# Five reorderings around the waits of TensorE in a two-block forward pass on one core: sums inside units, a chunked tail, split square sums, a double norm, pool products inside attention

## The reference, cut to what matters

```python
def reference(x, mem, ...):
    x = first_block(x, mem, ...)       # recurrence + fox attention, memory attention, MLP, final rmsnorm
    return second_block(x, c_2, ...)   # two layers, below

def second_block(x, c, ada_w, ada_b, ...):
    cond = jax.nn.silu(c)
    for layer in range(2):
        mod = cond @ ada_w[layer] + ada_b[layer]               # the conditioning: 1024 x 6144
        sh1, sc1, g1, sh2, sc2, g2 = jnp.split(mod, 6, axis=-1)
        h = modulate(rms_norm(x), sh1, sc1)
        y = pool_attention_mixer(h, ...) if layer % 2 == 0 else mlstm_mixer(h, ...)
        x = x + g1[:, None, :] * y
        h = modulate(rms_norm(x), sh2, sc2)
        x = x + g2[:, None, :] * swiglu(h, ffn_w1[layer], ffn_w3[layer], ffn_w2[layer])
    return x
```

## Time and profile before

| | |
|---|---|
| median of 3 runs | 2217.24 us (2216.86 to 2221.02) |
| the profiled execution, its own time | 2220.52 us |
| its span | 2218.8 us |
| PE busy in the span | 2095.2 us (94%) |
| DVE, ACT, POOL busy | 51%, 33%, 39% |
| mean granted TensorE clock | 0.976 of full |

### The profile page before, as it was taken

The page is one execution under the profiler, slowest core; times in us unless marked ns, Lnnn a source line. Parts: engine busy times, 40 slices in busy tenths (PEclk is TensorE's granted clock), DMA queues, the critical chain, the costliest instruction groups (busy, mean ns, idle before and its releaser), DMA issues.

```text
span 2218.8 us, 26605 instructions
## 1 busy us (share of the span) xinstructions
PE 2095.2 (94%) x10118; PEld 1694.5 (76%) x10118; DVE 1134.4 (51%) x1872; ACT 722.9 (33%) x975; POOL 861.7 (39%) x456
## 2 busy tenths in 40 slices
PE   6999898999899999989989999999999989999998
PEld 5877787876677878866477888887797777888887
DVE  4344556432788885457627676713664654111112
ACT  4343533333323132344523222223344323222221
POOL 2323423722344444422333444443435433444442
PEclk9999999999899999989999999999999999999999
DMA  4322003422355553231044555422232112222222
GB/s 135 105 71 82 29 1 114 155 73 87 123 190 181 174 175 95 95 109 38 1 133 139 175 179 189 151 91 81 95 117 96 38 57 76 95 95 95 95 90 81
DMA packets 225134, 233.15 MB, mean 105 GB/s; under 512 B 4211, under 2 KB 220100, under 8 KB 224908
## 3 DMA queue, kind: packets, MB, share of 16 engines
q1 hardware_dynamic: 225036, 231.81, 32.0%
HBM read 229.55 MB, written 2.24 MB: 104 GB/s over the span
## 4 chain that ended last, share of the span: by engine, by line
PE 81%; DVE 10%; ACT 3%; issue 3%; POOL 1%; DMA 1%; SPq 0%; DVEq 0%; ACTq 0%
PE ps L1918 20%; PE ps L1920 19%; PE ps L1919 19%; PE ps L1967 6%; PE ps L1972 3%; PE ps L2488 1%; ACT wH L714 1%; PE ps L2502 1%; PE ps L2065 1%; POOL wL L588 1%; DVE adacc L1560 1%; PE ps L2241 1%; DVE hnL L1231 1%; DVE T L1244 1%; PE ps L2172 1%
## 5 line engine op out<-in xcount | busy, mean ns | idle before, releaser
L588 POOL TENSOR_TENSOR wL<-raw,wH 128x1024 fp32r<-128x1024 f32 (+2 forms) x322 | 772.3, 2420 | 1199.8 <-ACT wH L714 1199.6
L714 ACT ACTIVATE wH<-raw 128x2048 fp32r<-128x2048 f32 (+2 forms) x161 | 302.5, 1879 | 517.0 <-PE ps L1920 382.9
L1918 PE MATMUL ps<-hnH,wH 128*128 128x512 f32 x1152 | 455.8, 396 | 3.0 <-POOL wL L588 3.0
L1920 PE MATMUL ps<-hnH,wL 128*128 128x512 f32 x1152 | 449.8, 390 | 0.0
L1919 PE MATMUL ps<-hnL,wH 128*128 128x512 f32 x1152 | 449.1, 390 | 0.0
L1560 DVE SCALAR_TENSOR_TENSOR adacc<-adaw,small,adacc 128x256 f32<-128x256 f32 x336 | 273.7, 815 | 12.0
L1918 PE MATMUL ps<-uH,wH 128*128 128x512 f32 x664 | 262.7, 396 | 5.2 <-issue 2.5
L1920 PE MATMUL ps<-uH,wL 128*128 128x512 f32 x664 | 260.3, 392 | 0.0
L1919 PE MATMUL ps<-uL,wH 128*128 128x512 f32 x664 | 260.2, 392 | 0.0
L1918 PEld LDWEIGHTS ps<-hnH,wH 128*128 128x128 f32 x1152 | 217.1, 188 | 48.0 <-issue 4.4
L1920 PEld LDWEIGHTS ps<-hnH,wL 128*128 128x128 f32 x1152 | 216.6, 188 | 46.1
(11 more groups left out here) (383 smaller groups left out, 3007.6 us busy)
## 6 DMA issues: line engine op xcount, KB each, us to landing
raw<-in_ffn_w_dram SPq DMA_DIRECT2D x60, 1024.0 KB, 5.3
adaw<-in_ada_w_dram SPq DMA_DIRECT2D x48, 1024.0 KB, 7.2
raw<-in_w_dram SPq DMA_DIRECT2D x32, 1024.0 KB, 5.3
raw<-in_w_in_dram SPq DMA_DIRECT2D x14, 1024.0 KB, 5.4
raw<-in_od_w_in_dram SPq DMA_DIRECT2D x12, 1024.0 KB, 5.4
raw<-in_w_xkv_dram SPq DMA_DIRECT2D x8, 1024.0 KB, 5.4
raw<-in_ffn_w_dram SPq DMA_DIRECT2D x8, 768.0 KB, 4.3
raw<-in_ev_w_in_dram SPq DMA_DIRECT2D x5, 1024.0 KB, 5.3
```

The source lines that it names most:

```text
L588: nc.gpsimd.tensor_tensor(wL[n % 2][:, k0:k1, 0:c], raw[n % 2][:, k0:k1, 0:c], wH[n % 2][:, k0:k1, 0:c].bitcast(F32), ALU.subtract).then_i ...
L714: nc.scalar.activation(wH[n % 2][:, 0:kc, 0:c], raw[n % 2][:, 0:kc, 0:c], ACT.Copy).then_inc(w_hi, 1)
L1918: nc.tensor.matmul(out_ap, wh, xh, start=first, stop=False)
L1920: return nc.tensor.matmul(out_ap, wl, xh, start=False, stop=last)
```

## The change

1. **Conditioning sums inside units.** `conditioning_sums` of group u-1 is called inside unit u, between its two blocks, or at chunk 4 where the unit goes chunk by chunk (u = 4 in the first MLP, u = 8 in the other). The last group of each pass stays behind its unit. The number of sums is the same.
2. **The tail of the mLSTM.** DVE finishes head 6 after four decay products of head 7, not six, and takes its steps in another order; PE transposes two heads ahead of each `out_rows` of head 7 and one behind, and the last three beside chunks 3, 5 and 6 of the first `od_out` unit (before: 1, 3 and 4). ACT rounds the first two transposed heads before it rounds the weights of `od_out`'s second unit. POOL waits until all heads are scaled before it goes on with weights.
3. **The last square goes to PE.** In every norm with square sums, `norm_add` for the last chunk is gone; `norm_sum` adds `sq` by a second matmul per token block.
4. **The double norm.** DVE works out both means first; ACT takes both roots, the second while DVE inverts the first. `msq` is now the whole second factor, broadcast first; `rootinv` is broadcast after it and has a semaphore of its own (`e_bc`).
5. **Pool products inside grid attention.** They run at steps 17, 19, 25 and 27; their scaling, rounding and remainders are at the next two steps of ACT and DVE. Attention's outputs go to banks 1 and 2, pool products to banks 0 and 3. The chunks' order of completion is given by two tables, and `ev_out` starts as soon as chunk 0 is there.

```diff
+MIX_OUT = (0, 3, 6, 7)
+MIX_POOL = (1, 2, 4, 5)
+POOL_STEP = (17, 19, 25, 27)
+OUT_BANK = {"cross": 0, "grid": 1}
...
@@ POOL
             gated_head(ML_H - 2)
             gated_head(ML_H - 1)
+            pool.wait_ge(n_h, ML_H)
             lows(AT["od_out"][0] + 1, AT["ff2_1"][0])
@@ ACT
-            high(n + 14)
             mixed_high(0)
             mixed_high(1)
+            high(n + 14)
...
@@ DVE residual_and_sums
-                norm_add(name, KC - 2, twice)
-                norm_add(name, KC - 1, twice)
+                    if j == KC - 2:
+                        norm_add(name, KC - 2, twice)
@@ DVE double norm
-            inverse_root("ev")
+            dve.wait_ge(root_done, NORMS["ev"] + 1)
+            dve.wait_ge(bc_done, NORMS["ev"])
+            chain(nc.vector.tensor_scalar(nt1, ps[6][:, 0:4], 1.0 / D, EPS, ALU.mult, ALU.add))
+            chain(nc.vector.tensor_scalar(nt2, ps[6][:, 4:8], 1.0 / D, None, ALU.mult))
+            nc.vector.scalar_tensor_tensor(out=nt3, in0=nt1, scalar=EPS, in1=nt2, op0=ALU.mult, op1=ALU.add).then_inc(e_ms, 1)
+            chain(nc.vector.reciprocal(rootinv, root))
+            newton(rootinv, nt1, nt2).then_inc(inv_done, 1)
...
-            chain(nc.vector.reciprocal(msq, root))
-            chain(newton(msq, nt1, nt2))
-            nc.vector.tensor_tensor(msq, msq, rootinv, ALU.mult).then_inc(e_inv, 1)
+            chain(nc.vector.reciprocal(msq, root2))
+            newton(msq, nt3, nt2).then_inc(e_inv, 1)
@@ DVE tail
-                    if x == 5 and h:
+                    if x == (3 if tail else 5) and h:
                         heads_out(h - 1, 1)
...
@@ PE norm_sum
-                    for tb in range(TB):
-                        ins = nc.tensor.matmul(ps[6][:, 4 * g + tb:4 * g + tb + 1], (ssum, gsum)[g][:, tb * P:(tb + 1) * P],
-                                               ones[:, 0:1], start=True, stop=True)
+                        nc.tensor.matmul(to, (ssum, gsum)[g][:, ts], ones[:, 0:1], start=True, stop=False)
+                        ins = nc.tensor.matmul(to, last[:, ts], ones[:, 0:1], start=False, stop=True)
@@ PE
+            def sums_inside(layer, i, u, chunkwise):
+                if u == 0:
+                    return {}
+                if chunkwise:
+                    return {"beside": lambda k: conditioning_sums(layer, i, u - 1) if k == KC // 2 else None}
+                return {"between": lambda: conditioning_sums(layer, i, u - 1)}
...
-            broadcast(rootinv, 4)
             broadcast(msq, 5).then_inc(bc_done, 1)
+            pe.wait_ge(inv_done, NORMS["ev"] + 1)
+            broadcast(rootinv, 4).then_inc(e_bc, 1)
...
+                    if kind == "grid" and s in POOL_STEP:
+                        pool_product(POOL_STEP.index(s))
...
-                feature_unit(n, uH, uL, need=all_chunks_of(Q0["ev_mix"]) if u == 0 else None, whole=True)
+                feature_unit(n, uH, uL, need=mixed if u == 0 else None, whole=True)
```

More of the change, by code:

```diff
@@ L267, in bass_block_pair @@
     nt2 = small[:, 176:180]
+    root2 = small[:, 180:184]
+    nt3 = small[:, 184:188]
     hnt = adab[:, 0:64]
@@ L993, in _ @@
             act.wait_ge(e_ms, 1)
-            nc.scalar.activation(root, nt1, ACT.Sqrt).then_inc(e_root, 1)
+            nc.scalar.activation(root2, nt3, ACT.Sqrt).then_inc(e_root, 1)
             norm_highs(Q0["ev_norm"], lambda j: mod[:, j:j + 1], AT["ev_in"][0] + 1)
@@ L1165, in _ @@
             head_roots(ML_H - 2)
+            mixed_high(4)
             head_roots(ML_H - 1)
-            for j in range(4, KC):
+            for j in range(5, KC):
                 mixed_high(j)
@@ L2400, in _, with pool_product, mixed @@
             feature_unit(n + 4, hnH, hnL, between=keys_twice)
-            attention("grid")
-            for j in range(4):
+            def pool_product(j):
                 pe.wait_ge(p_done, j + 1)
                 if j >= 2:
-                    pe.wait_ge(op_lo, Q0["ev_mix"] + 4 + j - 1)
-                nc.tensor.matmul(ps[2 + j % 2][:], wpool[:, j, :], pd[:, j, :], start=True, stop=True).then_inc(p_mm, 1)
+                    pe.wait_ge(op_lo, Q0["ev_mix"] + MIX_POOL[j - 2] + 1)
+                nc.tensor.matmul(ps[3 * (j % 2)][:], wpool[:, j, :], pd[:, j, :], start=True, stop=True).then_inc(p_mm, 1)
+            attention("grid")
+            def mixed(k):
+                return Q0["ev_mix"] + max((MIX_POOL + MIX_OUT)[:k + 1]) + 1
             for u, n in enumerate(range(*ranges("ev_out"))):
-                feature_unit(n, uH, uL, need=all_chunks_of(Q0["ev_mix"]) if u == 0 else None, whole=True)
+                feature_unit(n, uH, uL, need=mixed if u == 0 else None, whole=True)
             def gated_ffn(layer):
```

114 lines of the change are left out of this document (70 added, 44 removed).

## The result

| | median | runs | ratio to before, 95% interval |
|---|---|---|---|
| before, same chip | 2217.52 us | 2216.86 to 2221.02 | |
| changed | 2191.50 us | 2190.74 to 2196.67 | 0.9875 (0.9859 to 0.9891) |

The change makes the kernel 26 us faster; the forecast was 2191.0 us. The profiled execution took 2196.67 us by its own time (span 2194.9), 5.2 us above the median, so it too is read against its own time. The sum came out right, but several of its terms did not: parts 1 and 5 gave clearly more than I said, part 4 as much or a little more, and part 2 costs far more time than its term. The experiments are about that.

A forecast was written before the change was run, and what follows sets the result against it. PE was taken as the bound, busy 2095.2 of 2218.8 us. Terms -12.9 + 0.5 - 1.9 - 7.6 - 4.3 = -26.2 us gave 2194.3 us for the profiled execution, 2191.0 as median; range 2184.5 to 2202.

The forecast's parts named there:

- Part 1: Conditioning sums inside units: PE's waits for adacc and one half-clock stretch go, -12.9 us, between -7 and -13.9.
- no half clock at 589: First conditioning wait: the 3.4 us half-clock stretch at 589.5 us that follows it disappears, winning 1.7 us.
- Part 2: Last square by PE in the norms: four added matmuls eat DVE's saved addition, +0.5 us, between -1.2 and +3.9.
- The floor by ACT's table load: In a norm: ACT's table load and warming keep the root from coming more than 0.3 us sooner.
- Part 3: Double norm: fewer DVE operations, hidden second root, fewer transposes before scaling, -1.9 us, between -0.5 and -3.
- Part 4: Pool products inside grid attention: 10.0 us pause goes, 4.1 us added to attention; -7.6 us, between -4 and -8.5.
- (c): Rival: DVE and ACT hold attention, DVE the tail; pool term -4, tail -2, time 2197 us; chance 0.12.
- Part 5: mLSTM tail: new order lets od_out start and its first unit end sooner, -4.3 us, between -1.5 and -5.5.
- the two holds of DVE: mLSTM tail: POOL's gate products for heads 6 and 7 each hold DVE 1.1 us, 2.2 us less gain.
- (a): Rival: accumulator waits are DVE's pace and are only replaced; conditioning sums give -7, time 2197 us; chance 0.13.
- (d): Rival: moved sums stop their unit's second block, 0.85 us for each of 43, +36 us, 2240 us; chance 0.03.
- (b): Rival: half-clock stretches stay and move; two more of 6.8 us cost 6.8 us, time 2198 us; chance 0.14.

The follow-up runs named there:

- e2: Changed kernel with every conditioning sum behind its own unit again, all else kept: 2207.89 us (0.9937 of the kernel before).
- e6: Changed kernel with DVE adding the last square again (double norm: the last two), both roots still taken at once: 2186.10 us (0.9839).
- e5: Changed kernel with the old norms, both the last square by PE and the double norm's new order taken back: 2187.46 us (0.9853).
- e3: Changed kernel with pool products, scaling, rounding and remainders behind grid attention again, old banks and chunk order: 2199.45 us (0.9904).
- e4: Changed kernel with the mLSTM tail in its old order on DVE, PE, ACT and POOL, without POOL's new wait: 2200.51 us (0.9904).
- e7: Changed kernel with PE adding over ssum (and gsum) before it waits for the last square: 2184.11 us (0.9834).

## Why the prediction was right, and where it wasn't

| part | term | measured | from |
|---|---|---|---|
| 1, sums inside | -12.9 | -14.9 (medians of e2: -16.4) | ratios of e2; MLPs 375.2 and 377.4 to 363.3 and 374.4 |
| 2, last square | +0.5 | +4.4 (medians: +5.4, ratios: +6.9) | norms of e6 |
| 3, double norm | -1.9 | -2.1 (medians: -1.4, not clear of noise) | double norm of e6 against before; e5 against e6 |
| 4, pool products | -7.6 | -6.9 to -8.9 | e3, ratios (-7.5), medians (-8.0) and stretches |
| 5, tail | -4.3 | -7.5 to -9.0 | e4, ratios, medians; stretch -8.5 |

The total was right because the errors cancel, and that is luck: part 2 costs 4 to 6 us more than said, parts 1, 4 and 5 give 5 to 9 us more. By the medians the five measured terms add up to -29.4 (-16.4 + 5.4 - 1.4 - 8.0 - 9.0), where the two comparisons of the whole gave -26.0 and -29.0; by the ratios to -26.1, where they gave -27.8 and -28.9. So the parts add up as well as the runs can tell.

**Part 1.** The mechanism was right in every point: pitch 11.38, no half clock at 589, no other wait. The term was too small because it took the waits from the view that counts idle time. That view counts from the modelled end of the matmul ahead (0.39 us after its start), though the next could start after 0.23. From start to start the eight steps are 14.3 us together (one is 694.17 to 695.76 in the earlier trace rows); less 0.23 for each it is 12.5, and with the clock's 1.7 it is 14.2.

**Part 2** is the term that failed: +0.5 was taken, +4.4 or more came. Its price of eight instructions, 0.92 us against 0.79, was right at full clock (the root 0.2 us later, forecast 0.13). What was mis-sized is, first, the norms in which the clock falls early, so that the sums run at half clock: 16 more instructions are 3.4 us in the double norm, and about 1 us came on top in a single one. The prediction had the lower clock only at the range's end (+3.9). Second, it is the addition of chunk 6, which the prediction put beside PE's last block "at no cost" and which holds the last residual for 0.7 us where DVE is behind. The floor by ACT's table load was right, but it bounds a gain, not a loss.

**Part 3.** From the root to DVE's first scaling 5.16 us before (952.99 to 958.15), 3.55 after (945.09 to 948.64): the 1.6 us that were forecast.

**Part 4.** A step with a product is 0.86 us longer, not 1.03, so attention grew by 3.4 us, not 4.1; no stall by DVE, and `ev_out` at full clock from its start, as forecast. Rival (c) is out for attention.

**Part 5.** The new row was right: second direction 5.0 us after the first forecast, 5.5 measured, and in profiles without half clock there (e7) the first unit ends 21.65 us after the first row of head 7, against 21.0 forecast. Wrong was the row of before: after the transposes at 1800.26 four chunks were left, not one, so its unit ended at 1806.16 and not at 1802.0, and the 4.2 us of the difference are the greater part of the term's error. Of the two holds of DVE that the range allowed for, one was there (1771.42), and PE waits 0.82 us for head 5.

**The rivals.** (a) and (d) are excluded by the equal MLP stretches, (c) by the attention steps and by e4. (b) was right that the half-clock stretches stay and move. Behind the single norms they cost nothing, since PE isn't the bound there. Where PE's own work is the path they do: under the sums of the double norm and of a single norm, and in the mLSTM (226.9 us ahead of head 7 in the changed kernel, 220.5 in e5). Such stretches vary from execution to execution, and did not take the gain back.

## What to carry to other kernels

Cost an instruction that is moved to a faster engine by where it stands: the same matmuls cost nothing ahead of the last input's wait and some 5 us over five norms behind it, most where the clock had fallen. Take a wait's worth from the starts of successive matmuls, and count the work left after a landmark row instead of reading it off. When an order is changed to bring small DVE operations forward, ask what POOL streams beside them; here one wait on POOL carries 4.7 of the 6 to 7 us that the new tail gives.

## What the runs showed that I hadn't expected

- The same program gets its half-clock stretches at other places from run to run. In the double norm of the changed kernel the clock fell 2.4 us after the last unit matmul in one execution and 5.5 us in the other, 14.4 against 11.6 us.
- A one-column matmul of the sums takes 0.11 us an instruction at full clock and 0.213 at half: such work, though tiny, took nearly twice as long at half the clock.
- A first unit that consumes fresh chunks takes the same time whether 3 or 10 us at half clock stand at its start; the stretches of the MLPs are equal to 0.1 us in twelve profiles, with stretches of 3.4, 6.8 or 10.2 us at half clock around their start.
- Before the first norm, where nothing differs, executions differ by 5 us. A profile's span alone says nothing on changes below that; stretches do.
